# A two-layer diffusion-transformer kernel on one core: the scan's prologue moved by half a tile to a tile among the projections, its stores reordered, and a memset cut to one fifth

## The chip, the cores and the metric

The kernel runs on one core of a Trainium2 chip. The metric is the device time of one execution in microseconds; lower is better. The core has TensorE (matmuls, PE in the views), VectorE (DVE), ScalarE (ACT), GpSimd (POOL) and SyncE (SP), which here issues all the transfers. Each engine runs its own list of instructions in order, and they meet through semaphores.

## What is computed

The reference has two layers. Layer 0 mixes tokens by neighbourhood attention and a Hyena convolution, layer 1 by an RWKV-7 mixer that runs over the sequence in both directions; each layer has a SwiGLU network behind its mixer. The change lies in layer 1's mixer:

```
def rwkv_features(h, mu, w_rkv, w0, w1, w2, a0, a1, a2, g1, g2, k_k, k_a, readout):
    xx = 0.5 * (shift_prev(h) + shift_next(h)) - h
    mix = lambda i: h + xx * mu[i]
    k = mix(2) @ w_rkv[1]
    v = mix(3) @ w_rkv[2]
    ...
    kk = kk / jnp.maximum(jnp.sqrt(jnp.sum(jnp.square(kk), axis=-1, keepdims=True)), 1e-12)
    k_dir = k[None] * (1.0 + (a - 1.0) * k_a)
    if readout:
        r = mix(0) @ w_rkv[0]

def update(s, w_t, k_t, v_t, kk_t, a_t):
    sa = jnp.einsum('ebhvk,ebhk->ebhv', s, kk_t)
    return s * w_t[..., None, :] - sa[..., :, None] * (kk_t * a_t)[..., None, :] + v_t[..., :, None] * k_t[..., None, :]
```

There are 512 tokens and 256 context tokens, a width of 1024, and 16 heads of 64 in this mixer. Everything is in float32.

## The kernel before

A product with large weights is done in parts: each weight tile (128 output rows, 1024 inputs) is split by POOL into a high and a low half, and TensorE multiplies high by high, high by low and low by high. The mixer's three projections (value, key, receptance) are 24 such tiles, t = 0 to 23, eight each. A tile is eight steps k of TensorE; for receptance (t = 16 to 23) a step is three matmuls of 512 columns. For tile t: SP loads the weights (L2052) once tile t-4 is done, POOL splits them (L2184, L2186), TensorE multiplies (L1746), ACT copies the sum to one of three buffers (L1802), and SP stores it to DRAM (`keep`, L2046). In its loop SP issues the load of tile t together with `keep(t-6)`; the last six stores stand in a loop behind it.

Then the scan runs over eight pairs of heads. Its work for a pair has three parts, and round by round (`ROUNDS`) it does the back part of pair i, the front part of pair n = i+1 and the beginning of pair c = i+2. In time order for one pair:

- `kk`, `kr`: sums of the squared keys (TensorE L2450, needs the table `HONES`), their roots spread out by ACT (`kroot`, `kwide`, L2762, L2770), turned back by TensorE (L2583), and the product on DVE (`kmul`, L3029).
- `l00 l10`, `l01 l11`: two small low-rank products on TensorE (L2282), with tangents on ACT (`t00`, `t10`, ..., L2602), a gate on POOL (L2194) and prefix scans on DVE (L2803), which need the tables `RUN` and `MK`.
- exponentials and rates on ACT, products on DVE (`kin`, `ba_0`, `bt_0`, `ba_1`, `bt_1`, ..., L2808 to L2823), ending in `acc_0` on ACT (L2730).
- `A_0 A_1`: the gram matrices on TensorE (L2340), masked by DVE (L2830), sent out by SP (L2108) and brought back as 16x16 diagonal blocks (L2114), which POOL inverts by substitution (L2216, L2217). In pair 0, POOL also sets a buffer `XY` to zero (L2215) ahead of the last step. The inverses go out (L2118, L2122) and come back (L2126, L2131), and ACT and DVE expand them (L2656, L3035).
- the back part, which begins with `ta tx tb` on TensorE (L2307, L2299).

Each engine's list for the scan is a generator: a `next(scan)` in the projections' loop runs it up to its next `yield`. So the prologue (the beginning of pairs 0 and 1) is laid between projection tiles by hand. TensorE's five pieces are `kk`; `kr`; `l00 l10`; `l01 l11`; `A_0 A_1`. ACT's four are the keys' scaling and squares; `kroot kwide`; the first tangents; exponentials up to `acc_0`. SP's five are `keys_of(0) values_of(0)`; `HONES` and five small tables; `RUN` and `MK`, which wait until the stores of two buffers have landed; `queries_of(0)`; and `lora_of(1)` with the grams' way out and back. POOL's two are the gates, and an empty piece. DVE runs the scan behind its mixing, with no pieces. What is left of each list runs behind tile 23.

SP's order around the loads of the tables is this:

```
                if t >= 6:
                    keep(t - 6)
                if t in (17, 19, 21):
                    next(scan)
```

Of the kernel before, what the change touches and what calls it, by code (L numbers as in the profile page):

```python
# [84 lines left out]
def hybrid_dit_kernel(nc, a, out):  # L85
# [3 lines left out]
    with ctx:  # L89
# [1650 lines left out]
        def projections_pe(pe, scan):  # L1740

            def products(t, d, k):
                w_hi, w_lo = WH[:, t % SLOTS, k, :], WRR[:, t % SLOTS, k, :]
                for p, (wt, x) in enumerate(((w_hi, d.hi), (w_hi, d.lo), (w_lo, d.hi))):
                    for h0, h1, b in (((0, HALF, 0), (HALF, T, 1)) if d.n == T else ((0, L, 0),)):
                        last = nc.tensor.matmul(PS[:, kept_bank(t) + b, 0:h1 - h0], wt, x[:, k, h0:h1],  # L1746
                                                start=k + p == 0, stop=k == CT - 1 and p == 2)
                return last

            for k in range(CT):  # L1750
                pe.wait_ge(input_split, SPLIT_MIX + k + 1)
                for t in range(2):
                    if k == 0:
                        pe.wait_ge(lora_hid, 2)
                        pe.wait_ge(weights_split, SPLITS["value"] + t + 1)
                    last = products(t, value, k)
                    if k == CT - 1:
                        last.then_inc(slots_used, 1)
            for t, (w, d, m) in enumerate(PROJECTIONS):
                if t < 2:  # L1760
                    continue
                if t < SLOTS:
                    pe.wait_ge(lora_hid, t + 1)
                else:
                    pe.wait_ge(kept_tile, t - SLOTS + 1)
                pe.wait_ge(weights_split, SPLITS["value"] + t + 1)
                for k in range(CT):
                    if m == 0:
                        pe.wait_ge(input_split, SPLIT_MIX + d.at + k + 1)
                    last = products(t, d, k)  # L1770
                last.then_inc(slots_used, 1)
                if t in (16, 17, 18, 20):
                    next(scan)
                if t == 17:
                    next(scan)

        def projections_act(act, scan):

            def upper(d, k):
                act.wait_ge(mix_raw, d.at + k + 1)  # L1780
                if d is key and k == 0:
                    act.wait_ge(slots_used, 4 * (LORA + 1))
                if d is recept and k == 0:
                    act.wait_ge(slots_used, 4 * value.base + CT)
                nc.scalar.activation(d.hi[:, k, 0:d.n], RAW[:, (d.at + k) % 2, 0:d.n], ACT.Copy).then_inc(input_hi, 1)

            u = 4 * LORA
            for k in range(CT):
                if k == 2:
                    act.wait_ge(slots_used, u + 3)  # L1790
                    nc.scalar.activation(as_halves(TH), halves(4), ACT.Tanh).then_inc(lora_hid, 1)
                if k == 6:
                    act.wait_ge(slots_used, u + 4)
                    nc.scalar.activation(as_halves(AH), halves(6), ACT.Copy).then_inc(lora_hid, 1)
                upper(value, k)
            for t, (w, d, m) in enumerate(PROJECTIONS):
                if w < 2:
                    upper((key, recept)[w], m)
                act.wait_ge(slots_used, 4 * value.base + t + 1)
                if t >= 3:  # L1800
                    act.wait_ge(kept_out[t % 3], 16 * (t // 3))
                nc.scalar.activation(as_halves(kept_at(t), d.n), halves(kept_bank(t), d.n), ACT.Copy)\  # L1802
                  .then_inc(kept_tile, 1)
                if t in (15, 16, 17, 18):
                    next(scan)

        def mixes_sp(sp):
# [102 lines left out]
        TOKK, KINT, BVT, XY, OOS, NE = carve(ARENA[3], [2 * T, 2 * T, 2 * T, 5 * T, 5 * T, 2 * T])  # L1910
# [18 lines left out]
        XY = XY.rearrange("p (a h j t) -> p a h j t", a=5, h=2, j=6)  # L1929
# [111 lines left out]
        def projections_sp(sp, scan):  # L2041
# [14 lines left out]
                    next(scan)  # L2056
            for t in range(len(PROJECTIONS) - 6, len(PROJECTIONS)):
                keep(t)
                if t in (18, 20):
                    next(scan)  # L2060

        H2 = [slice(0, 64), slice(64, 128)]
# [115 lines left out]
        def projections_pool(pool, scan):  # L2178

            for t in range(len(PROJECTIONS)):  # L2180
# [3 lines left out]
                nc.gpsimd.tensor_copy(hi, raw).then_inc(weights_hi, 1)  # L2184
                pool.wait_ge(weights_hi, SPLITS["value"] + t + 1)
                nc.gpsimd.tensor_tensor(lo, raw, hi.bitcast(F32), ALU.subtract).then_inc(weights_split, 1)  # L2186
                if t in (20, 21):
                    next(scan)

        def scan_pool(pool):  # L2190
            sub = Chain(pool, sub_step)
# [11 lines left out]
            def substitute(n):  # L2203
                pool.wait_ge(blk_back, 32 * n + 32)
                for s in range(BK - 1):
# [6 lines left out]
                    prod = strided(PROD[:, 0:1], (256, 2), (BK, rows), (1, cols))  # L2212
                    if n == 0 and s == BK - 2:
                        pool.wait_ge(slots_used, 4 * value.base + 3 * CT)
                        sub.link(nc.gpsimd.memset(XY[:, :, :, :, :].rearrange("p a h j t -> p (a h j t)"), 0.0))  # L2215
                    sub.link(nc.gpsimd.tensor_tensor(prod, coef, done, ALU.mult))  # L2216
                    ins = nc.gpsimd.tensor_tensor(rest, rest, prod, ALU.subtract)  # L2217
                    if s < BK - 2:
# [1056 lines left out]
```

## Time and profile before

| | us |
|---|---|
| three timed runs | 2462.48, 2462.98, 2466.24 (median 2462.98) |
| the profiled execution | 2464.82 |
| its span, from the first to the last instruction | 2463.0 |
| TensorE busy | 2216.2 (90% of the span) |
| VectorE, ScalarE, GpSimd busy | 942.2, 688.3, 852.2 |

The profile is one execution. Its page gives the busy time of each engine and groups of instructions by line; the trace behind it answers questions on a stretch: what ran when on one engine (the timeline), what ended the idle time in front of an instruction (in brackets), and busy time and granted TensorE clock by stretch. All times are microseconds from the start of the span.

### The profile page before, as it was taken

The numbers are of one execution on the slowest core, as the hardware profiler recorded it, in microseconds if no ns is written. First come the engines' busy times: TensorE is split into PE (matmuls) and PEld (weight loads), VectorE is DVE, ScalarE is ACT, GpSimd is POOL, SyncE is SP. The second block draws the span as 40 slices with busy tenths as digits, with TensorE's granted clock in tenths as the row PEclk, the third lists the DMA queues.
The fourth block names the chain that finished last, engine by engine and source line by source line (L and its number), as shares of the span: only waits on it lengthen the run. The fifth ranks groups of instructions, "written<-read, shape, count | busy, mean of one in ns | idle before, by whom it ended". The sixth has DMA issues, their size and how long they took to land. (4 is left out here: it accounts for less than half of the span.)

```text
span 2463.0 us, 50823 instructions
## 1 busy us (share of the span) xinstructions
PE 2216.2 (90%) x22528; PEld 1842.0 (75%) x22528; DVE 942.2 (38%) x1500; ACT 688.3 (28%) x1059; POOL 852.2 (35%) x692
## 2 busy tenths in 40 slices
PE   5899989989699999999958998888888887999997
PEld 3788765555399999999926996777776665888785
DVE  3102265990320000022289214777777524000123
ACT  4110166421320000022232123555555223101112
POOL 2132300000233443434306445333333243666662
PEclk8999999999799999999979999999999988999998
DMA  6555530001012112111112444323233131222221
GB/s 247 214 192 215 194 135 18 1 8 69 26 52 68 60 60 68 60 60 60 45 37 77 118 131 116 65 56 59 56 63 62 23 117 55 94 94 94 85 99 64
DMA packets 175508, 210.32 MB, mean 85 GB/s; under 512 B 124791, under 2 KB 133751, under 8 KB 168152
## 3 DMA queue, kind: packets, MB, share of 16 engines
q1 hardware_dynamic: 175320, 207.49, 27.3%
q8 instruction: 157, 2.57, 0.4%
q14 instruction: 31, 0.25, 0.0%
HBM read 184.65 MB, written 22.81 MB: 84 GB/s over the span
## 5 line engine op out<-in xcount | busy, mean ns | idle before, releaser
L254 POOL CAST TMP_r<-WR 128x1024 fp32r<-128x1024 f32 x120 | 127.2, 1060 | 718.4 <-DMA WR<-in_ffn_w_dram 437.1
L273 PE MATMUL PS<-H_r,TMP_r 128*128 128x384 f32 (+1 forms) x1088 | 330.2, 359 | 11.6 <-DVE Y_r L490 11.6
L273 PE MATMUL PS<-Y_r,TMP_r 128*128 128x384 f32 (+1 forms) x1088 | 329.9, 358 | 3.7 <-DVE H_r L490 3.7
L256 POOL TENSOR_TENSOR WR_r<-WR,TMP_r 128x1024 fp32r<-128x1024 f32 x120 | 289.2, 2410 | 9.6
L413 DVE TENSOR_TENSOR P<-TMP,PS 128x768 f32 (+1 forms) x44 | 36.1, 821 | 562.5 <-PE PS L273 562.5
L273 PEld LDWEIGHTS PS<-H_r,TMP_r 128*128 128x128 f32 x1088 | 202.5, 190 | 28.3 <-DVE Y_r L490 12.6
L273 PEld LDWEIGHTS PS<-Y_r,TMP_r 128*128 128x128 f32 x1088 | 201.3, 189 | 19.3 <-DVE H_r L490 4.0
L273 PE MATMUL PS<-H_r,WR_r 128*128 128x384 f32 x736 | 191.6, 342 | 0.0
L396 ACT ACTIVATE TMP<-PS 128x768 f32<-128x768 f32 (+1 forms) x44 | 31.0, 705 | 526.1 <-PE PS L273 526.1
L590 PE MATMUL PS<-H_r,TMP_r 128*128 128x384 f32 x704 | 151.9, 338 | 3.2 <-DVE H_r L628 2.2
L273 PE MATMUL PS<-Y_r,WR_r 128*128 128x512 f32 x352 | 139.2, 396 | 0.0
L273 PEld LDWEIGHTS PS<-H_r,WR_r 128*128 128x128 f32 x736 | 133.4, 189 | 0.0
L590 PEld LDWEIGHTS PS<-H_r,TMP_r 128*128 128x128 f32 x704 | 125.5, 189 | 3.8 <-DVE P L413 2.5
L1746 PE MATMUL PS<-P_r,TMP_r 128*128 128x384 f32 (+1 forms) x448 | 114.2, 347 | 6.7 <-POOL WR_r L2186 4.3
L2216 POOL TENSOR_TENSOR scan_small<-scan_small 96x30 f32<-96x30 f32 (+7 forms) x120 | 49.7, 414 | 191.3 <-DMA scan_small<-gram_dram 182.6
L590 PE MATMUL PS<-Y_r,TMP_r 128*128 128x512 f32 x352 | 109.7, 393 | 2.2 <-DVE Y_r L628 2.2
L266 POOL TENSOR_TENSOR WR_r<-WR,TMP_r 128x1024 fp32r<-128x1024 f32 x44 | 107.2, 2437 | 3.5
L1629 PE MATMUL PS<-H_r,TMP_r 128*128 128x384 f32 x352 | 93.4, 347 | 8.6 <-POOL WR_r L256 8.6
L264 POOL CAST TMP_r<-WR 128x1024 fp32r<-128x1024 f32 x44 | 47.3, 1074 | 154.7 <-DMA WR<-in_down_dram 154.7
L2184 POOL CAST TMP_r<-WR 128x1024 fp32r<-128x1024 f32 x24 | 42.1, 1756 | 151.3 <-DMA WR<-in_rw_w_rkv_dram 151.3
L628 DVE TENSOR_TENSOR H_r<-P,H_r 128x768 fp32r<-128x768 f32 x44 | 44.2, 1043 | 125.7 <-ACT H_r L621 125.7
L1746 PE MATMUL PS<-P_r,WR_r 128*128 128x384 f32 (+1 forms) x320 | 91.3, 350 | 0.0
(327 smaller groups left out, 4468.0 us busy)
## 6 DMA issues: line engine op xcount, KB each, us to landing
WR<-in_ffn_w_dram SPq DMA_DIRECT2D x88, 512.0 KB, 3.4
TMP<-in_mod_w_dram SPq DMA_DIRECT2D x40, 1024.0 KB, 4.8
WR<-in_down_dram SPq DMA_DIRECT2D x44, 512.0 KB, 3.4
WR<-in_mix_w_in_dram SPq DMA_DIRECT2D x24, 512.0 KB, 6.9
WR<-in_rw_w_rkv_dram SPq DMA_DIRECT2D x24, 512.0 KB, 4.2
P<-in_mod_w_dram SPq DMA_DIRECT2D x4, 2048.0 KB, 22.0
vkr_dram<-extra SPq DMA_DIRECT2D x16, 384.0 KB, 4.8
scan_front<-vkr_dram SPq DMA_DIRECT2D x16, 384.0 KB, 3.6
```

Source lines behind the costliest of these rows:

```text
L254: nc.gpsimd.tensor_copy(hi, raw).then_inc(weights_hi, 1)
L256: nc.gpsimd.tensor_tensor(lo, raw, hi.bitcast(F32), ALU.subtract).then_inc(weights_split, 1)
L264: nc.gpsimd.tensor_copy(hi, raw).then_inc(weights_hi, 1)
L266: nc.gpsimd.tensor_tensor(lo, raw, hi.bitcast(F32), ALU.subtract).then_inc(weights_split, 1)
L273: last = nc.tensor.matmul(PS[:, bank + b, 0:h1 - h0], w, x[:, h0:h1], start=k + p == 0, stop=k == CT - 1 and p == 2)
L413: nc.vector.tensor_tensor(as_halves(dst, d.n), as_halves(GATE[:, u, 0:d.n], d.n), halves(4 * u + 2, d.n), ALU.mult).then_inc(d.unit_free, 1)
L590: last = nc.tensor.matmul(PS[:, bank, 0:h1 - h0], w[:, at:at + 128], x[:, q % 4, h0:h1], start=k + p == 0, stop=k == FT - 1 and p == 2)
L628: nc.vector.tensor_tensor(d.lo[:, q % 4, :], P[:, q % FT, 0:d.n], d.hi[:, q % 4, :].bitcast(F32), ALU.subtract).then_inc(hid_split, 1)
L1629: last = nc.tensor.matmul(PS[:, 2 * u + b, 0:HALF], w, x[:, HALF * b:HALF * b + HALF], start=k + p == 0, stop=k == CT - 1 and p == 2)
L1746: last = nc.tensor.matmul(PS[:, kept_bank(t) + b, 0:h1 - h0], wt, x[:, k, h0:h1], start=k + p == 0, stop=k == CT - 1 and p == 2)
L2184: nc.gpsimd.tensor_copy(hi, raw).then_inc(weights_hi, 1)
L2216: sub.link(nc.gpsimd.tensor_tensor(prod, coef, done, ALU.mult))
```

## The change

It moves where the pieces of the prologue are run, and cuts one memset.

- TensorE: `kk` moves from behind tile 16 to behind step k = 3 of tile 16; `kr` and `l00 l10` from behind tile 17 to behind tile 16; `l01 l11` from behind tile 18 to behind step k = 3 of tile 17; `A_0 A_1` from behind tile 20 to behind tile 19.
- ACT: its four pieces move from behind the evictions of tiles 15, 16, 17, 18 to behind those of 15, 15, 16, 17.
- SP: `queries_of(0)` stays behind `keep(18)`, and the piece with the grams, which stood behind `keep(20)`, follows it at once, ahead of `keep(19)` to `keep(23)`. The pieces at t = 17, 19, 21 stay.
- POOL: the gates move from behind the split of tile 20 to behind that of tile 19. The memset of `XY` covers one of its five parts, `XY[:, 4]`.

```diff
--- before.py
+++ after.py
@@ -1768,10 +1768,12 @@
                     if m == 0:
                         pe.wait_ge(input_split, SPLIT_MIX + d.at + k + 1)
                     last = products(t, d, k)
+                    if t in (16, 17) and k == 3:
+                        next(scan)
                 last.then_inc(slots_used, 1)
-                if t in (16, 17, 18, 20):
+                if t in (16, 19):
                     next(scan)
-                if t == 17:
+                if t == 16:
                     next(scan)
 
         def projections_act(act, scan):
@@ -1801,7 +1803,9 @@
                     act.wait_ge(kept_out[t % 3], 16 * (t // 3))
                 nc.scalar.activation(as_halves(kept_at(t), d.n), halves(kept_bank(t), d.n), ACT.Copy)\
                   .then_inc(kept_tile, 1)
-                if t in (15, 16, 17, 18):
+                if t in (15, 16, 17):
+                    next(scan)
+                if t == 15:
                     next(scan)
 
         def mixes_sp(sp):
@@ -2056,7 +2060,8 @@
                     next(scan)
             for t in range(len(PROJECTIONS) - 6, len(PROJECTIONS)):
                 keep(t)
-                if t in (18, 20):
+                if t == 18:
+                    next(scan)
                     next(scan)
 
         H2 = [slice(0, 64), slice(64, 128)]
@@ -2184,7 +2189,7 @@
                 nc.gpsimd.tensor_copy(hi, raw).then_inc(weights_hi, 1)
                 pool.wait_ge(weights_hi, SPLITS["value"] + t + 1)
                 nc.gpsimd.tensor_tensor(lo, raw, hi.bitcast(F32), ALU.subtract).then_inc(weights_split, 1)
-                if t in (20, 21):
+                if t in (19, 20):
                     next(scan)
 
         def scan_pool(pool):
@@ -2212,7 +2217,7 @@
                     prod = strided(PROD[:, 0:1], (256, 2), (BK, rows), (1, cols))
                     if n == 0 and s == BK - 2:
                         pool.wait_ge(slots_used, 4 * value.base + 3 * CT)
-                        sub.link(nc.gpsimd.memset(XY[:, :, :, :, :].rearrange("p a h j t -> p (a h j t)"), 0.0))
+                        sub.link(nc.gpsimd.memset(XY[:, 4].rearrange("p h j t -> p (h j t)"), 0.0))
                     sub.link(nc.gpsimd.tensor_tensor(prod, coef, done, ALU.mult))
                     ins = nc.gpsimd.tensor_tensor(rest, rest, prod, ALU.subtract)
                     if s < BK - 2:
```

## Rows read from the trace of the kernel before

**Rows 1.** The page, its first part: busy time of each engine.

```profile
PE 2216.2 (90%) x22528; PEld 1842.0 (75%) x22528; DVE 942.2 (38%) x1500; ACT 688.3 (28%) x1059; POOL 852.2 (35%) x692
```

**Rows 2.** Busy time by stretch: length, PE, PEld, DVE, ACT, POOL, clock, DMA share, GB/s.

```profile
1315.00:1514.50 199.50, 191.50 (x1099) 178.80 (x1098) 78.01 (x80) 48.18 (x68) 91.34 (x59) 0.98 0.39 112
1514.50:1540.10 25.60, 14.73 (x313) 12.15 (x312) 9.22 (x15) 12.40 (x19) 18.63 (x28) 0.89 0.36 74
```

**Rows 3.** Timeline of TensorE: start, length, line, operation, count, idle before.

```profile
1461.79 0.39 PE L1746 MATMUL PS<-P_r,TMP_r 128*128 128x512 f32 x1
...
1467.62 1.47 PE L2450 MATMUL PS<-scan_front 128*128 128x2 f32 x12 [0.19 <-DMA scan_front<-in_headones_dram]
...
1474.52 0.82 PE L2583 MATMUL PS<-ident,scan_front 128*128 128x128 f32 x6
1476.43 1.56 PE L2282 MATMUL PS<-TMP,scan_small 64*128 64x384 f32 x8 [1.09 <-issue]
...
1496.17 1.85 PE L2340 MATMUL PS<-scan_tokens,scan_front 64*64 64x64 f32 x96
...
1514.49 0.93 PE L2329 MATMUL PS<-scan_front,scan_tokens 64*64 64x64 f32 x48
...
1531.93 1.56 PE L2282 MATMUL PS<-TMP,scan_small 64*128 64x384 f32 x8 [1.38 <-DVE scan_front L2857]
1540.13 1.56 PE L2307 MATMUL PS<-scan_back,scan_tokens 64*64 64x64 f32 x48 [6.64 <-ACT scan_back L2656]
```

**Rows 4.** Timeline of VectorE.

```profile
1483.38 4.00 DVE L2803 TENSOR_TENSOR_SCAN scan_front<-extra,scan_front 128x768 f32<-128x768 f32 x2 [7.05 <-DMA extra<-in_grammask_dram]
...
1495.36 1.68 DVE L2815 SCALAR_TENSOR_TENSOR scan_front<-scan_front 128x768 f32<-128x768 f32 x1
...
1547.45 1.79 DVE L2797 TENSOR_TENSOR scan_small<-scan_back,PS 128x768 f32<-128x768 f32 x2
```

**Rows 5.** Timeline of ScalarE.

```profile
1470.13 0.84 ACT L2770 ACTIVATE scan_front<-scan_small 128x768 f32<-128x768 f32 x1 [0.58 <-DVE scan_small L3017]
...
1537.95 2.13 ACT L2656 ACTIVATE scan_back<-scan_back,scan_small 128x384 f32<-128x384 f32 x4 [9.01 <-DMA scan_back<-inv_dram]
...
1541.50 0.90 ACT L2602 ACTIVATE scan_front<-PS,PC 128x768 f32<-128x768 f32 x1
```

**Rows 6.** Timeline of GpSimd.

```profile
1512.17 0.23 POOL L2216 TENSOR_TENSOR scan_small<-scan_small 96x30 f32<-96x30 f32 x1 [12.22 <-DMA scan_small<-gram_dram]
...
1526.40 3.31 POOL L2215 MEMSET scan_back<- 128x3840 f32 x1
```

**Rows 7.** Timeline of SyncE: its DMA issues.

```profile
1462.83 0.43 SPq L2092 DMA_DIRECT2D scan_front<-in_headones_dram  x1
...
1474.71 0.33 SPq L2052 DMA_DIRECT2D WR<-in_rw_w_rkv_dram  x1
1475.08 0.43 SPq L2046 DMA_DIRECT2D vkr_dram<-extra  x1
1479.81 0.33 SPq L2100 DMA_DIRECT2D extra<-in_run_dram  x1
...
1503.21 3.35 SPq L2108 DMA_DIRECT2D gram_dram<-scan_tokens  x4
```

**Rows 8.** DMA issues, 1455 to 1545 us: count, KB, median us to landing.

```profile
extra<-in_grammask_dram SPq DMA_DIRECT2D x1, 128.0 KB, 3.1
...
scan_front<-in_headones_dram SPq DMA_DIRECT2D x1, 64.0 KB, 4.7
```

**Rows 9.** Lines L2803 and L2808: duration ns min/median/max, first and last start.

```profile
L2803 DVE TENSOR_TENSOR_SCAN scan_front<-extra,scan_front x16: 1726/1758/2354, 1483.4 to 1887.7; 128x768 f32<-128x768 f32 x16
...
L2808 DVE TENSOR_TENSOR scan_tokens<-scan_front x16: 936/940/3146, 1488.3 to 1894.1; 128x756 f32<-128x756 f32 x16
```

**Rows 10.** Busy time by stretch, around the start of round 0; columns as in rows 2.

```profile
1538.00:1539.00 1.00, 0.00 (x0) 0.00 (x0) 0.00 (x0) 1.00 (x3) 0.00 (x0) 0.56 0.75 67
...
1544.00:1545.00 1.00, 1.00 (x48) 1.00 (x47) 1.00 (x1) 0.72 (x1) 1.00 (x1) 0.53 0.72 261
```

## The prediction, made before the change was run

> **What bounds the kernel now.** The page says that TensorE is busy for 90% of the span [rows 1], but that is an average. I read it by stage next [rows 2]: the projections (to 1514.5 us) keep TensorE busy 191.5 of 199.5 us, the passage into the scan (1514.5 to 1540.1) only 14.7 of 25.6. All that the change touches lies in these two. Eight scan rounds follow, each hanging on the one before, so I take a shift of round 0 as a shift of the end. The question is: when can round 0 (`ta`, L2307) start?
>
> TensorE runs in order, and two chains end there. The **inversion chain**: SP sends the masked grams at 1503.21 [rows 7], POOL substitutes from 1512.17 [rows 6], the result goes out again, ACT expands it from 1537.95 [rows 5], and `ta` starts at 1540.13. The **front chain**: after the last projection tile TensorE does all of head pair 0's turns and grams and pair 1's `kk`, `kr` and `l00 l10`; it starts at 1514.49, and its last link starts at 1531.93 and takes 1.5 us [rows 3]. So before, 6.64 us of idle lie behind the front chain [rows 3], and the inversion chain decides. The change shortens the inversion chain; that can win 6.6 us at most, if the front chain doesn't move. My claim is that the front chain moves, and by more.
>
> **Part 1, `kk` in the middle of tile 16.** It needs `HONES`. SP issues that load at 1462.83, in the step behind the end of tile 15 [rows 7], and it takes 4.7 us to land [rows 8]: 1467.5. Before, `kk` stood behind tile 16 and waited 0.19 us for it [rows 3]. A tile of 24 matmuls takes 5.4 us (from 1461.79 on, with its last matmul's pipeline 5.6). Now TensorE reaches `kk` after 12 of them, at 1464.6, and stands still until 1467.6 with tile 16's second half and all later tiles queued behind. Idle grows by 2.9 us. `kk` holds TensorE for 1.3, the second half takes 3.0: tile 16 ends at 1471.9, where it ended at 1467.4.
>
> **Part 2, `kr` and `l00 l10` behind tile 16, `l01 l11` in tile 17.** ACT's `kwide`, which `kr` needs, is through at 1471.0 [rows 5], and is no earlier now, since `kk` isn't. `kr` (0.8 us), the wait for DVE's product (1.1, as before) and `l00 l10` (1.5) [rows 3] now lie ahead of tile 17, which starts at 1475.2. Its halves (2.8 and 3.0) with `l01 l11` (1.5) between them end at 1482.5. Before, it had none of this ahead of it and ended at 1474.7. So **tile 17 ends 7.8 us later**: 2.9 of stall, and 3.4 and 1.5 of small work moved ahead of it. Moved work by itself costs TensorE nothing.
>
> **Part 3, the load that hangs on tile 17.** SP's step t=21 is not changed: it waits for the end of tile 17, issues a weight load and `keep(15)`, and the scan's next step waits for that store to land before it loads `RUN` and `MK` over its buffer. Before: 1474.71, 1475.08, then 1479.81 [rows 7] and 3.1 us from `MK`'s issue to its landing [rows 8]. DVE's two prefix scans need both and had waited 7.05 us for them [rows 4]. Now the same steps run 7.8 us later: `RUN` goes out at 1487.6, and the scans start at **1491.2 instead of 1483.4**. The gates on POOL come earlier (behind tile 19's split, not 20's), but DVE wasn't waiting for them.
>
> **Part 4, the grams behind tile 19.** `A_0` and `A_1` need `bt_0` and `bt_1` of DVE. `bt_1` ended 13.7 us after the scans' start, at 1497.04 [rows 4]. Now that is 1491.2 + 13.7 = 1504.9. The unknown is how far POOL's weight splits stretch DVE. Before, the two scans took 4.00 where the median is 1.76 each, and `bt_1` 1.68 where products of its size take 0.94 [rows 4, 9]: 1.2 us on this path. One product was stretched from 0.94 to 3.15, 2.2 us. Two splits still fall here (tiles 22 and 23, on the second scan and on `ba_0`). I take the old sum; without any stretch it is 1503.7, with one in full 1505.9, with two 1508.1. TensorE has ended tile 19 at 1493.3 and idles until `bt_0` at about 1503. `A_1`, half of the grams' 1.85 us, takes 0.9, and tile 20 starts at 1506.0 with the handover. Before, the grams ran from 1496.17 to 1498.0 [rows 3] and three tiles came behind them; now four do. The end of tile 23 moves by 8.0 + 5.4 = **13.4 us**.
>
> **The clock.** Behind the 6.64 us of idle before `ta` the granted clock falls to half, the lower of the two levels (1.2 GHz): the slice from 1538 has 0.56, that from 1544 still 0.53 [rows 10], so the lower level lasts some 4.4 us into the work. The new idle of 9 us is longer. Half of those 4.4 us is lost where the work is dense; `A_0` and the wait for `bt_1` hide part. I take 1.2 us, with 0 and 2.2 as bounds. Sum for tile 23: **14.6 us**. The Trainium skill (TensorE: Matmul & The Clock Gate, Part 1) says that an idle array falls to half its clock and sustained work frees it again; the trace agrees (0.53 and 0.56). It speaks against any edit that opens a gap in dense work; a clock that stayed up would leave the sum at 2467.8.
>
> **Part 5, what follows tile 23.** The rest of the front chain keeps its length: its links wait for tile 23, for the last store, and for `keys_of(1)`, whose load SP issues behind that store. So `l00 l10` of pair 1 starts at 1531.9 + 14.6 = 1546.5, ACT's first tangent at 1548.0 instead of 1541.50 [rows 5], and `ta` at 1548.0 instead of 1540.13. The old idle is used up. From there it is DVE's first sweep (1547.45 before, right behind a scan [rows 4]) that counts: tangent 0.9, eviction of `ta` 0.8, tangent 0.9, gate 0.85, scan 1.8 put it at 1553.4. **Round 0's dense part comes 6.0 us later.** `ta`, `tx` and `tb` ran at the low clock before and now run mostly warm; that is why it is 6.0 and not 7.9.
>
> **Part 6, the inversion chain, now covered.** ACT runs its fourth step ahead of evicting tile 18. It waits there for the scans, and the evictions of tiles 18 and 19 are queued behind it until `acc_0` (about 1506.5); their banks are needed only by tiles 22 and 23, later. `keep(18)` waits for them too. SP issues it, `queries_of(0)` and two small loads (2.0 us) and sends the grams at about 1509, not 1503.2. `keep(19)` to `keep(23)` queue behind the grams' return, and have time, since their tiles end later. Substitution starts 9.0 us behind the sending [rows 6, 7], at 1518. The memset shrinks to a fifth: 3.31 us for 3840 columns [rows 6] becomes 0.7, which saves 2.6. The expansion could begin at 1541.3, but ACT's `kwide` for pair 1, ahead of it, ends at 1543.4. `ta` at 1548.0 waits for neither. So the memset edit is worth nothing here; with the front chain on time it would be worth its 2.6 us.
>
> **Rival A, the move works (2456.4).** If neither load is late, the prologue runs a tile earlier: the inversion chain gains 5.4 and 2.6, the front chain doesn't move, and `ta` gains the 6.6 us of idle. For it: TensorE's work is the same in sum. Against it: `HONES` and `RUN` stay issued behind the ends of tiles 15 and 17, and DVE's wait of 7.05 us for the latter is in the trace. It decides if the scans start before 1483. Chance 0.12.
>
> **Rival B, the delay is half hidden (2466.6).** No stretch (-1.2) and no cold clock (-1.2): tile 23 moves 12.2 and round 0 3.6. Further slack in round 0 would take it towards 2463. For it: one stretched product, of 3.15 us, lay where DVE waited for ACT anyway. Against it: both splits are still to be done. Chance 0.33.
>
> **Rival C, more contention (2472.4).** `RUN` and `MK` now go out half a microsecond ahead of tile 22's weight load and a store: up to 1.6 us more, if they land like the 4.7 us of rows 8. With one stretch in full (+1.0) and the full cold price (+1.0) that is 3.4 to 3.6 us over the main case; with two stretches 2474.6. Chance 0.12.
>
> By the Trainium skill (GPSIMD Engine Reference, the table at its head) GpSimd shares its memory interface with DVE where a DVE instruction has two inputs in SBUF, as the scans and products here have. The stretched product agrees.
>
> **How the numbers follow.** The profiled span is 2463.0 us (that execution took 2464.8; the median of three is 2462.98, so I add to the median as it is): 2463.0 + 6.0 = **2469.0 us**, +0.24%. This case by itself spans 2467 to 2472 and has chance 0.43. The range that should hold 8 in 10 takes in rival B with its slack and all of C but its end: 2459 to 2474. About 0.2% (4.9 us) is what a measurement of this kernel can tell from no change. The main case and C lie above it, B inside, A below: slower 0.55, same 0.33, faster 0.12.
>
> **What the profile after would show.** Right: a wait of 3 us ahead of L2450 within tile 16; `RUN` issued near 1487.6 and L2803 starting near 1491; TensorE idle some 9 us ahead of L2340; the last L1746 near 1528; hardly any idle ahead of `ta`; a memset of 0.7 us. Wrong: L2803 before 1484, L2340 right behind tile 19, or several microseconds of idle left ahead of `ta`, which would mean that the inversion chain still decides.

## The result, and the profile after

| | before | after |
|---|---|---|
| median | 2462.48 us | 2474.28 us |
| lowest and highest (7 runs each) | 2454.77, 2466.24 | 2467.21, 2478.70 |
| the profiled execution, its span | 2464.82, 2463.0 | 2470.45, 2468.7 |

The ratio is 1.0046 [1.0030, 1.0061]: the change makes the kernel **11.3 us slower**, between 7.4 and 15.0. The forecast was +6.0. The direction and the way were right; the size was about half of the measured one, and the median of after lies at the upper end of the range (2474), 0.3 us above it. It is also outside the 2467 to 2472 that the main case spans by itself: as a number it is nearest to rival C (2472.4, at its end 2474.6).

The profiled execution of after, 2470.45, is close to the 2469.0 forecast, but that is no confirmation. The work upstream of the change varies between executions. Tile 16 starts at 1461.79 before [rows 3], and after it starts at 1456.14, 5.65 us sooner, with nothing changed ahead of it. All distances below are therefore taken **from the start of tile 16 of the same execution**.

TensorE in the profile of after, the same places as in rows 3 (start, length, line, operation, shape, count, idle before and its releaser; these lines of the kernel are numbered 5 higher):

```profile
1456.14 0.39 PE L1746 MATMUL PS<-P_r,TMP_r 128*128 128x512 f32 x1
...
1462.22 1.47 PE L2455 MATMUL PS<-scan_front 128*128 128x2 f32 x12 [3.16 <-DMA scan_front<-in_headones_dram]
...
1465.11 0.63 PE L1746 MATMUL PS<-Y_r,TMP_r 128*128 128x512 f32 x1
1465.54 0.63 PE L1746 MATMUL PS<-P_r,WR_r 128*128 128x512 f32 x1
...
1467.98 0.81 PE L2588 MATMUL PS<-ident,scan_front 128*128 128x128 f32 x6
...
1500.48 1.56 PE L2345 MATMUL PS<-scan_tokens,scan_front 64*64 64x64 f32 x48 [10.77 <-DVE scan_front L2820]
1502.34 1.56 PE L2345 MATMUL PS<-scan_tokens,scan_front 64*64 64x64 f32 x48 [0.30 <-DVE scan_front L2820]
1503.83 0.79 PE L1746 MATMUL PS<-P_r,TMP_r 128*128 128x512 f32 x1
...
1525.98 0.39 PE L1746 MATMUL PS<-P_r,WR_r 128*128 128x512 f32 x1
...
1535.37 2.54 PE L2455 MATMUL PS<-scan_front 128*128 128x2 f32 x12 [2.41 <-ACT scan_front L2763]
...
1540.50 2.48 PE L2372 MATMUL PS<-scan_tokens,scan_front 64*64 64x64 f32 x96
...
1545.52 2.67 PE L2287 MATMUL PS<-TMP,scan_small 64*128 64x384 f32 x8 [1.38 <-DVE scan_front L2862]
1548.12 1.41 PE L2312 MATMUL PS<-scan_back,scan_tokens 64*64 64x64 f32 x48
```

Three of the forecast signs stand in it. `kk` waits 3.16 us in the middle of tile 16, where it had waited 0.19 [rows 3]. The grams wait 10.77 us behind tile 19, where there was no wait. Behind the front chain `ta` starts at 1548.12 with no idle at all, where there had been 6.64 us [rows 3]. And VectorE shows where the grams' wait is from:

```profile
1487.43 3.41 DVE L2808 TENSOR_TENSOR_SCAN scan_front<-extra,scan_front 128x768 f32<-128x768 f32 x2 [17.64 <-DMA extra<-in_grammask_dram]
1491.74 3.95 DVE L2813 TENSOR_TENSOR scan_tokens<-scan_front 128x756 f32<-128x756 f32 x2 [0.91 <-ACT scan_front L2611]
1495.62 1.78 DVE L2817 SCALAR_TENSOR_TENSOR scan_front<-scan_front 128x768 f32<-128x768 f32 x1
1497.44 2.98 DVE L2820 SCALAR_TENSOR_TENSOR scan_front<-scan_front 128x768 f32<-128x768 f32 x1
1500.35 0.94 DVE L2817 SCALAR_TENSOR_TENSOR scan_front<-scan_front 128x768 f32<-128x768 f32 x1
1501.33 0.96 DVE L2820 SCALAR_TENSOR_TENSOR scan_front<-scan_front 128x768 f32<-128x768 f32 x1
...
1554.20 1.79 DVE L2802 TENSOR_TENSOR scan_small<-scan_back,PS 128x768 f32<-128x768 f32 x2
```

The scans wait 17.64 us for their tables (7.05 in rows 4). SyncE's issues name the step that sends the tables late: the weight load and the store behind the end of tile 17, and the wait for that store.

```profile
1457.18 0.43 SPq L2097 DMA_DIRECT2D scan_front<-in_headones_dram  x1
...
1478.86 0.33 SPq L2056 DMA_DIRECT2D WR<-in_rw_w_rkv_dram  x1
1479.23 0.43 SPq L2050 DMA_DIRECT2D vkr_dram<-extra  x1
1484.01 0.33 SPq L2105 DMA_DIRECT2D extra<-in_run_dram  x1
```

What stood at 12.9, 13.3 and 18.0 us behind the start of tile 16 [rows 7] now stands at 22.7, 23.1 and 27.9.

The windows of after (length, PE, PEld, DVE, ACT, POOL, clock, DMA share, GB/s) hold something that the forecast had missed:

```profile
1464.00:1466.00 2.00, 2.00 (x7) 1.51 (x6) 0.57 (x2) 0.84 (x1) 0.33 (x1) 0.50 0.00 0
```

Most of the second half of tile 16 runs at a granted clock of 0.50, the lower of the two levels, with matmuls 0.43 us apart instead of 0.23. The 3.16 us ahead of `kk` are paid as a wait, and then more is lost to the low clock, in the densest part of the kernel.

### The profile page after: what moved, and what is told of

It is laid out like the page before. It is cut to its first block and busy times, and to the rows that moved or that the text cites. A ratio compares the mean times of both kernels' runs of the same rounds, so it can differ in the third digit from the quotient of the medians.

```text
span 2468.7 us, 50823 instructions
## 1 busy us (share of the span) xinstructions
PE 2213.2 (90%) x22528; PEld 1843.5 (75%) x22528; DVE 943.7 (38%) x1500; ACT 688.6 (28%) x1059; POOL 848.1 (34%) x692
## 5 line engine op out<-in xcount | busy, mean ns | idle before, releaser
L273 PE MATMUL PS<-H_r,TMP_r 128*128 128x384 f32 (+1 forms) x1088 | 331.1, 360 | 11.1 <-DVE Y_r L490 11.1
L396 ACT ACTIVATE TMP<-PS 128x768 f32<-128x768 f32 (+1 forms) x44 | 31.1, 706 | 524.8 <-PE PS L273 524.8
## 6 DMA issues: line engine op xcount, KB each, us to landing
P<-in_mod_w_dram SPq DMA_DIRECT2D x4, 2048.0 KB, 21.6
```

What stands on the lines that cost most here:

```text
L273: last = nc.tensor.matmul(PS[:, bank + b, 0:h1 - h0], w, x[:, h0:h1], start=k + p == 0, stop=k == CT - 1 and p == 2)
```

## Where the 12.4 us of the profile come from

All in microseconds behind the start of tile 16:

| | before | after | moved | forecast |
|---|---|---|---|---|
| scans start | 21.6 | 31.3 | +9.7 | +7.8 |
| grams done, next tile starts (21 before, 20 after) | 36.2 | 47.7 | +11.5 | +8.0 |
| last matmul of tile 23 starts | 52.4 | 69.8 | +17.5 | +14.6 |
| `l00 l10` of pair 1 start | 70.1 | 89.4 | +19.2 | +14.6 |
| `ta` starts | 78.3 | 92.0 | +13.6 | +7.9 |
| first sweep on DVE | 85.7 | 98.1 | +12.4 | +6.0 |

The first sweep is DVE's first product of round 0 (L2797 before, L2802 after). From there on the two kernels take the same within some 1 us (915.6 us to the end of the span before, 914.5 after), so the row of the sweep is the row to read.

## The experiments

Three theories stood at the start. **Late loads**: `HONES` and `RUN` stay where they were, and the moved pieces wait for them. **Inversion chain**: it still sets the start of `ta`, as it did before. **Moved work**: the small pieces cost something by being cut into the tiles. A fourth, **low clock**, that part of the time is lost to matmuls at the lower level, came with the profile of after. Each kernel was timed beside the kernel before on the same chip, 5 rounds; "sweep" is how far the first sweep has moved against the profile of before, and "ratio" is the timed one. A sweep comes from one execution. The change measured a second time, **e13_change_again**, shows how much that is worth:

> The changed kernel once more, for a second profile and a second ratio, taken with the same runs of the kernel before as the three others. The part of the front chain behind tile 23, up to l00 l10 of pair 1, took 19.5 us in its first profile, 17.8 before the change and 16.0 to 18.8 in other versions, with the granted clock at half in more or fewer of its pieces. If that is a matter of where the clock happens to fall, it will differ again here, by up to 2 us, with the same program; the stall ahead of kk (3.0), the scans' start (31) and the gap ahead of the grams (10.8) will be the same. The ratio to before again 1.003 to 1.006.

Measured: 1.0045 [1.0028, 1.0062], 11.1 us, with the sweep at +10.3, where the first profile had +12.4. The ratios agree to 0.2 us, the two profiles differ by 2. TensorE again, in this second profile:

```profile
1463.39 1.47 PE L2455 MATMUL PS<-scan_front 128*128 128x2 f32 x12 [2.86 <-DMA scan_front<-in_headones_dram]
...
1501.46 1.56 PE L2345 MATMUL PS<-scan_tokens,scan_front 64*64 64x64 f32 x48 [10.58 <-DVE scan_front L2820]
...
1536.23 1.86 PE L2455 MATMUL PS<-scan_front 128*128 128x2 f32 x12 [1.98 <-ACT scan_front L2763]
...
1545.97 1.56 PE L2287 MATMUL PS<-TMP,scan_small 64*128 64x384 f32 x8 [1.38 <-DVE scan_front L2862]
```

The waits are the same within 0.3 us. What differs is the tail: `kk` of pair 1 takes 1.86 instead of 2.54 and `l00 l10` 1.56 instead of 2.67. So single profiles are good to some 2 us here, and smaller differences between them are not read.

The table of all kernels; positions are us behind the start of tile 16.

| kernel | scans start | last matmul of tile 23 | `ta` | sweep moved | ratio |
|---|---|---|---|---|---|
| before | 21.6 | 52.4 | 78.3 | | |
| the change | 31.3 | 69.8 | 92.0 | +12.4 | 1.0046 [1.0030, 1.0061] |
| e13_change_again | 30.9 | 69.7 | 89.9 | +10.3 | 1.0045 [1.0028, 1.0062] |
| e1_hones_early | 26.5 | 65.9 | 84.9 | +5.3 | 1.0030 [1.0016, 1.0044] |
| e2_run_early | 21.3 | 59.7 | 80.0 | +0.4 | 0.9995 [0.9984, 1.0007] |
| e3_both_early | 16.6 | 56.2 | 77.2 | -2.4 | 0.9990 [0.9978, 1.0002] |
| e4_grams_after_20 | 31.2 | 64.4 | 85.8 | +7.4 | 1.0026 [1.0013, 1.0039] |
| e5_full_memset | 31.1 | 69.9 | 90.1 | +10.6 | 1.0039 [1.0022, 1.0055] |
| e6_memset_alone | 21.8 | 52.5 | 77.0 | -1.3 | 0.9995 [0.9982, 1.0008] |
| e7_stores_alone | 21.6 | 52.7 | 77.0 | -1.4 | 0.9991 [0.9977, 1.0004] |
| e12_stores_and_memset | 21.6 | 52.3 | 73.9 | -4.4 | 0.9988 [0.9975, 1.0001] |
| e9_loads_early_grams_20 | 16.9 | 51.9 | 72.4 | -5.9 | 0.9967 [0.9954, 0.9980] |
| e10_before_all_but_pe | 17.7 | 51.8 | 72.3 | -7.2 | 0.9963 [0.9948, 0.9979] |
| e11_gaps_filled | 31.7 | 71.2 | 88.7 | +9.1 | 1.0035 [1.0022, 1.0049] |

### The load of HONES one step sooner

e1_hones_early is the change with one number altered; the step with `HONES` now stands behind the end of tile 14, not 15:

```diff
-                if t in (17, 19, 21):
+                if t in (17, 18, 21):
                     next(scan)
```

> The changed kernel, with SP's step that loads HONES moved from t = 19 to t = 18, so that the table is there when TensorE reaches kk in the middle of tile 16. RUN and MK stay behind tile 17. Front-chain theory (the end of the front chain on TensorE sets round 0, and the stall inside tile 16 and the low clock behind it are 4.8 of its delay): no stall ahead of kk, tile 16's second half at full clock, the scans start 26.5 us behind the start of tile 16 (31.3 in the changed kernel, 21.6 before), and the whole runs 4.8 us faster than the change, which leaves it about 6.5 us slower than before. Inversion-chain theory (the late sending of the grams sets round 0): the grams go out 4.8 us earlier too, so the same total, but TensorE is idle for several us ahead of ta. Rival that TensorE loses by interrupting a tile's accumulation: kk still costs more than its 1.3 us, and less than 2 us come back.

Measured: sweep +5.3, ratio 1.0030, 7.4 us. By the ratios 3.9 us came back (the two intervals overlap), by the profiles 5 (from the second profile of the change) to 7. `kk` does not wait (TensorE of e1):

```profile
1463.88 1.50 PE L2455 MATMUL PS<-scan_front 128*128 128x2 f32 x12
1468.09 0.82 PE L2588 MATMUL PS<-ident,scan_front 128*128 128x128 f32 x6
```

Its first row and its second are 4.21 us apart; in the change the same two are 5.76 apart (1462.22 and 1467.98). The difference, **1.6 us, is the price of the low clock** in tile 16's second half, since this kernel's clock is 1.00 there (window, columns as above). It repeats: the distance is 5.75 or 5.76 us in all five profiles in which `kk` waits some 3 us in the middle of tile 16 (the change twice, e2, e4, e5), and 4.20 or 4.21 in the three in which it doesn't wait there (e1, e3, e9).

```profile
1463.00:1465.00 2.00, 2.00 (x15) 1.65 (x14) 0.00 (x0) 1.98 (x2) 0.00 (x0) 1.00 0.76 266
```

The wait and the low clock together are 4.7 us, and the scans come 4.8 sooner than in the change. The wait ahead of the grams is as long as it was (10.76): early or late, tile 19 and the scans move together, since the load of `RUN` hangs on tile 17. Cutting tile 16 in two costs next to nothing by itself: of the 4.21 us `kk` takes 1.4, and the second half of the tile 2.8, like the first.

### The loads of RUN and MK one step sooner

```diff
-                if t >= 6:
+                if t >= 6 and t != 21:
                     keep(t - 6)
-                if t in (17, 19, 21):
+                if t == 20:
+                    keep(15)
+                if t in (17, 19, 20):
                     next(scan)
```

> The changed kernel, with the store of tile 15 issued at t = 20 behind that of tile 14, and RUN and MK loaded in that step instead of t = 21. HONES stays late. Front-chain theory: the stall in tile 16 stays (3 us, and 1.8 of low clock), but the scans start about 20.6 us behind the start of tile 16 instead of 31.3, the gap of 10.8 us ahead of the grams shrinks to under 1, tile 23 ends about 12 us earlier than in the change, and round 0 starts 15 us earlier: about 2 us faster than before. Inversion-chain theory: the grams go out earlier by as much, and the same comes out. Rival that the load of RUN was no cause: nothing comes back.

Measured: sweep +0.4, ratio 0.9995, 1.2 us faster than before, with an interval that takes in 1. Against the change some 12 us came back by either measure (+11.3 to -1.2; +12.4 to +0.4). This is the largest single part of the loss, and what was put right is SyncE's step, which the change does not touch. TensorE of e2:

```profile
1464.36 1.47 PE L2457 MATMUL PS<-scan_front 128*128 128x2 f32 x12 [2.86 <-DMA scan_front<-in_headones_dram]
...
1491.77 0.93 PE L2347 MATMUL PS<-scan_tokens,scan_front 64*64 64x64 f32 x48
1495.71 0.93 PE L2347 MATMUL PS<-scan_tokens,scan_front 64*64 64x64 f32 x48 [3.02 <-DVE scan_front L2822]
```

`A_0` no longer waits. `A_1` still waits 3.02 for `bt_1`, and yet it runs at the full clock (0.93 us).

### Both loads sooner

e3_both_early is e2 with `(17, 18, 20)`.

> The changed kernel with both loads early (HONES at t = 18, the store of tile 15 and RUN and MK at t = 20). Front-chain theory: no stall in tile 16, scans some 16 us behind the start of tile 16, no gap ahead of the grams, tile 23 ends where it ended before, and round 0 starts right behind the front chain, with the old idle of 6.6 us ahead of ta used up: 6 to 8 us faster than before (2455). It can't be more than about 8.5. If the inversion chain is what sets round 0, idle is left ahead of ta and the gain is smaller.

Measured: sweep -2.4 and 0.9990 [0.9978, 1.0002], 2.5 us with an interval that takes in 1, less than was expected. The waits for both loads are gone (`kk` has none), and the scans start 5.0 us sooner than before. What is late next is `A_1`. TensorE and VectorE of e3:

```profile
1485.46 0.93 PE L2347 MATMUL PS<-scan_tokens,scan_front 64*64 64x64 f32 x48
1489.25 1.56 PE L2347 MATMUL PS<-scan_tokens,scan_front 64*64 64x64 f32 x48 [2.86 <-DVE scan_front L2822]
```

```profile
1481.12 2.36 DVE L2819 SCALAR_TENSOR_TENSOR scan_front<-scan_front 128x768 f32<-128x768 f32 x1 [0.73 <-ACT scan_front L2626]
1483.51 0.96 DVE L2822 SCALAR_TENSOR_TENSOR scan_front<-scan_front 128x768 f32<-128x768 f32 x1
1484.39 1.79 DVE L2819 SCALAR_TENSOR_TENSOR scan_front<-scan_front 128x768 f32<-128x768 f32 x1
1486.21 2.98 DVE L2822 SCALAR_TENSOR_TENSOR scan_front<-scan_front 128x768 f32<-128x768 f32 x1
```

The four products before `A_1` take 8.1 us; 0.95 is what each takes undisturbed (`ba_1` and `bt_1` of after). GpSimd splits weights beside three of them. `A_1` then runs at the low clock (1.56 instead of 0.93), and the beginning of tile 20 too: 2.86 + 0.6 + 0.5 makes 4.0, and tile 23 is 3.9 us later than in before. In e2 the same piece waited 3.02 us and kept the full clock, so a wait of this length does not always cost a low clock; what decides it was not found. The loads early are not sufficient: with `A_0 A_1` behind tile 19 the product chain on DVE ends some 3 us too late. This kernel is also the test of rival A, the change with neither load late: it gives 2.5 us and not the rival's 6.6.

### The grams behind tile 20, as they were

e4_grams_after_20 is the change with the loads late and this edit; e9 has the early loads as well.

```diff
-                if t in (16, 19):
+                if t in (16, 20):
                     next(scan)
```

> The changed kernel, with TensorE's grams behind tile 20, where they were before, and all else as in the change. Tells the two chains apart: the grams can't run earlier than DVE's products allow, so SP sends them at the same time, but one more tile fills the gap in front of them. Front-chain theory: the gap shrinks from 10.8 to about 5 us, tile 23 and round 0 come 5.5 to 6 us earlier, so that it is 5 to 6 us slower than before. Inversion-chain theory: the sending of the grams and with it round 0 stay where they are, and it stays 11 us slower than before.

Measured: the wait ahead of `A_0` falls from 10.77 to 5.39, a tile's length; sweep +7.4; ratio 1.0026, 6.4 us. By the ratios 4.9 us came back, by the profiles 2.9 to 5.0. The gap is shorter by one tile, and by no more. The run also tells the two chains apart. SyncE sends the grams 50.1 us behind the start of tile 16, where the change has 50.5, and still `ta` comes 6.2 us sooner (4.1 against the second profile of the change): in the change the front chain sets its start and not the inversion chain.

> The kernel with both loads early, and TensorE's grams behind tile 20 as before the change. With the grams behind tile 19, A_1 had waited 2.9 us for bt_1 and ran at the low clock, and tile 23 ended 3.9 us later than before the change. Front-chain theory: the wait is gone, tile 23 ends where it did before the change (52.7 us behind the start of tile 16), nothing is idle ahead of ta, and DVE's first sweep comes 77 to 79 us behind the first receptance matmul, where it was 85.4 before and 83.1 with the grams behind tile 19: 6 to 8 us faster than before. If the inversion chain decides by now, idle is left ahead of ta and it is 2 to 4 us faster only.

Measured: 0.9967 [0.9954, 0.9980], **8.1 us faster than before**; sweep -5.9. No piece that TensorE runs among the projections waits for a load, and the grams do not wait for DVE:

```profile
1495.95 1.63 PE L2347 MATMUL PS<-scan_tokens,scan_front 64*64 64x64 f32 x96
```

### The kernel before, with everything but the moves on TensorE, ScalarE and GpSimd

e10 is the kernel before with e3's edit of SyncE's loop, SyncE's last two pieces together, and the small memset:

```diff
                 keep(t)
-                if t in (18, 20):
+                if t == 18:
+                    next(scan)
                     next(scan)
...
-                        sub.link(nc.gpsimd.memset(XY[:, :, :, :, :].rearrange("p a h j t -> p (a h j t)"), 0.0))
+                        sub.link(nc.gpsimd.memset(XY[:, 4].rearrange("p h j t -> p (h j t)"), 0.0))
```

> The kernel before with the change's two parts on the inversion chain (the grams sent ahead of the last stores, the small memset) and both loads early, but with no piece of the prologue moved on TensorE, ACT and POOL. If the half-tile steps themselves are worth something, this is slower than the version with them and both loads early (grams behind tile 20). Front-chain theory: it is as fast, 5 to 8 us faster than before, since the scans start some 19 us behind tile 16's start (21.6 before), the grams go out some 5 us earlier and the memset gives 2.6, up to the front chain's end. Rival: the scans wait for POOL's gates, which come late, and it stays within 3 us of before.

Measured: 0.9963 [0.9948, 0.9979], **9.1 us faster than before**, with a sweep of -7.2; the lowest ratio here. It and e9 differ by the moves of `kk`, `kr`, `l00 l10`, `l01 l11` alone (and their gates and exponentials), and their intervals overlap almost wholly: these moves have no gain of their own that was measured. TensorE and VectorE of e10:

```profile
1494.98 1.63 PE L2343 MATMUL PS<-scan_tokens,scan_front 64*64 64x64 f32 x96
...
1530.46 2.93 PE L2285 MATMUL PS<-TMP,scan_small 64*128 64x384 f32 x8 [1.38 <-DVE scan_front L2860]
1533.32 1.17 PE L2310 MATMUL PS<-scan_back,scan_tokens 64*64 64x64 f32 x48
```

```profile
1478.68 4.81 DVE L2806 TENSOR_TENSOR_SCAN scan_front<-extra,scan_front 128x768 f32<-128x768 f32 x2 [3.57 <-POOL scan_front L2197]
```

The scans now wait 3.57 us for GpSimd's gate and no longer for a load. That is not seen on TensorE: the grams run in one block with no wait. `ta` follows the front chain directly, so the inversion chain is no longer the bound; the front chain is, with `l00 l10` at the low clock (2.93 us where 1.56 is the full-clock time).

### The memset and the stores

e5_full_memset is the change with the whole of `XY` set to zero again.

> The changed kernel with the whole memset of before (3.3 us and not 0.7). Front-chain theory: the inversion chain has some 2 to 6 us to spare in the changed kernel, so it makes no difference to the change (within 1 us; 11 us slower than before). Inversion-chain theory: 2.6 us slower than the change.

Measured: 1.0039 [1.0022, 1.0055], sweep +10.6: no difference from the change can be told, as the forecast's Part 6 has it. With the front chain late the memset's length is covered.

On the kernel before the inversion chain is the bound, so there both edits should count. e6 has the memset's edit alone, e7 the order of SyncE's pieces alone, e12 both.

> The kernel before with the small memset alone. Before the change the inversion chain decides, with 6.6 us of idle on TensorE ahead of ta. Two-chain theory: the memset takes 0.7 us instead of 3.3, the idle ahead of ta shrinks by 2.6 and it is 2.6 us faster than before. Rival (the transfers of the inverses decide, or POOL's last steps aren't on the path): no difference.

> The kernel before with the grams sent ahead of the last stores alone. Before, SP came to the grams at 41.2 us behind the first receptance matmul, after two stores and two small loads that waited for ACT's late evictions, while the first masked gram was ready at about 39. Two-chain theory: the grams go out about 2 us earlier, substitution starts 2 us earlier, and it is 2 us faster than before. Rival: the stores now behind the grams delay the load of the next keys, and nothing is gained.

> The kernel before with the change's two parts on the inversion chain together: the grams ahead of the last stores and the small memset, and no piece moved on TensorE, ACT and POOL. Two-chain theory: the gains add, 2 + 2.6 = 4.6 us faster than before, with some 2 us of idle left ahead of ta. It tells how much of the 8 to 9 us of the version that also has its loads early is due to these two parts: about half.

Measured: the sweep moves by -1.3, -1.4 and -4.4 us, the ratios say -1.2, -2.2 and -3.0, each with an interval that takes in 1. So neither edit has a gain clear of the noise, alone or with the other. The forecast's "worth its 2.6 us" for the memset is neither shown nor ruled out: e6's profile gives 1.3, e12 against e7 gives 3.0, and the timed interval of e6 runs from 4.4 us faster to 2.0 slower. In e6's execution part of the gain was lost on the way. SyncE in before and in e6, the way out and back of the inverses:

```profile
1531.56 0.81 SPq L2118 DMA_DIRECT2D inv_dram<-scan_small  x2
...
1533.73 2.08 SPq L2126 DMA_DIRECT2D scan_back<-inv_dram  x2
```

```profile
1529.69 0.82 SPq L2118 DMA_DIRECT2D inv_dram<-scan_small  x2
...
1533.03 1.97 SPq L2126 DMA_DIRECT2D scan_back<-inv_dram  x2
```

Behind tile 16's start the first of these rows is at 69.8 and 67.3, so 2.4 us did arrive there; the last is at 71.9 and 70.7, and 1.3 is left. The return goes out 3.3 us behind the store instead of 2.2. Why the store's way took longer in this execution is not settled. With both edits the idle ahead of `ta` is down to 0.81 us, waiting for ScalarE, and the front chain is next.

### The gaps filled with work that keeps TensorE busy

e11_gaps_filled is the change with transposes of the identity put where TensorE would idle: 20 ahead of `kk`, 70 ahead of `A_0`. Their results are overwritten by what follows.

```diff
+                    if c == 0:
+                        for _ in range(20):
+                            nc.tensor.transpose(PS[:, b, 0:128], ident[:, :], ident[:, :])
...
+                    if n == 0:
+                        b = front("A_0", n)
+                        for _ in range(70):
+                            nc.tensor.transpose(PS[:, b, 0:128], ident[:, :], ident[:, :])
```

> The changed kernel with TensorE's two new gaps filled by transposes of the identity whose results are overwritten: 20 ahead of kk in tile 16 and 70 ahead of A_0, in the bank that comes next. No wait is shortened, so it tells the low clock's price from that of the waits. Theory: the granted clock stays at the full level, tile 16's second half takes 2.7 us and not 4.4 (1.8 back), A_1 and tile 20's first matmuls another 1.3; together 3 us faster than the change, 8 us slower than before. If the clock's fall has another cause than TensorE's idleness, nothing comes back.

Measured: 1.0035 [1.0022, 1.0049], 8.6 us, sweep +9.1. TensorE and the windows of e11 in tile 16:

```profile
1464.54 2.40 PE L2569 MATMUL PS<-ident 128*128 128x128 f32 x20
1467.66 1.50 PE L2455 MATMUL PS<-scan_front 128*128 128x2 f32 x12 [0.72 <-DMA scan_front<-in_headones_dram]
...
1473.45 0.82 PE L2595 MATMUL PS<-ident,scan_front 128*128 128x128 f32 x6
...
1500.14 9.71 PE L2502 MATMUL PS<-ident 128*128 128x128 f32 x70 [4.96 <-ACT scan_front L2614]
1509.78 1.63 PE L2345 MATMUL PS<-scan_tokens,scan_front 64*64 64x64 f32 x96
```

```profile
1465.00:1467.00 2.00, 1.94 (x18) 1.70 (x16) 0.00 (x0) 0.78 (x1) 0.61 (x1) 1.00 0.98 340
...
1470.00:1472.00 2.00, 2.00 (x6) 1.53 (x6) 0.15 (x1) 0.84 (x1) 0.00 (x0) 0.50 0.00 0
```

In tile 16 the theory fell in the form it was put. Only 0.72 us of idle is left, TensorE is busy in the records, and still the clock drops to 0.50 and the second half takes as long (`kk` to `kr`: 5.79 us, against 5.76 in the change and 4.21 in e1). Narrow matmuls back to back did not hold the clock there. So e1 shows that the low clock goes away with the wait for the load, and that TensorE's idleness in it is the cause is not shown. Ahead of the grams they did bring it back: the second filler waited 4.96 us for ScalarE to read its bank out, ran 70 transposes in 9.71, and the grams (1.63 for all 96, where the change needs 1.56 for 48) and tile 20 ran at the full clock. But it overran: `bt_0` had ended at 1506.5 and `A_0` starts at 1509.78. So tile 23 comes 1.4 us later than in the change. In this profile the sweep is sooner all the same, since the front chain takes 16.0 us (last matmul of tile 23 to `l00 l10`), the shortest of all kernels: 17.8 before, 19.5 and 18.7 in the two profiles of the change. By the ratios its 8.6 us and the change's 11.3 and 11.1 have overlapping intervals, so that the fillers gain anything is not shown.

## Why the prediction was right, and why its size was not

**Right.** The reading that two chains end at `ta`, and that the front chain moves by more than the 6.64 us of idle [rows 3] ahead of it; e4 shows that it sets `ta` in the change. (That the idle is all that can be won fits e9 and e10 by their profiles, 5.9 and 7.2, and by their timed intervals, which begin at 4.9 and 5.2 us.) The wait of 2.9 us for `HONES` (3.16 and 2.86 measured). `RUN` hanging on tile 17, shown by e2, which gives 12 us back with SyncE's step alone. The grams' idle ("some 9 us", measured 10.77). Part 6: the memset worth nothing in this kernel (e5), `ta` with no idle ahead. (SyncE sent the grams 50.5 us behind the start of tile 16 where Part 6 has 47.2, which stayed covered.) Rival A, that neither load is late, is out, and its 6.6 us would not have come either: e3, with both loads on time, gains 2.5 us by its ratio, since `A_1` then waits for DVE. Only with the grams back behind tile 20 as well do 8.1 us come (e9).

**Too small.** The forecast for the sweep was +6.0, the profile has +12.4. Term by term:

- **Part 1 left the clock out: +1.6.** It counted what an idle of 9 us does to the clock and took the 2.9 us ahead of `kk` as a plain wait. e1 puts the price at 1.6 us. The stall itself is 0.2 longer than forecast, and tile 17 is longer by 0.2 for its extra handover. Together: scans +9.7 instead of +7.8.
- **Part 4, the products: +1.2.** From the start of the scans to the end of `bt_1` it took 14.9 us, not 13.7. The forecast's sum with one product stretched in full (+1.0) comes within 0.2 us of that, but it was put in rival C, and belonged in the main case. In the trace the stretch is spread: 3.95 us for the two products of L2813, 1.78 for `ba_0`, 2.98 for `bt_0`, while the scans (3.41) and `bt_1` (0.96) took less than before.
- **The clock behind the gap: as forecast.** `A_1` takes 0.6 more and tile 20 0.5 more at the low level, 1.1 us against 1.2. Here tile 23 stands at +17.5 instead of +14.6.
- **Part 5 said that the front chain keeps its length: +1.8.** From tile 23's last matmul to `l00 l10` it was 17.8 before and is 19.5 here, 18.7 in the second profile. Its links are the same. `kk` takes 1.0 longer (2.54 in one profile, 1.86 in the other, 1.50 at the full clock) and the grams behind it 0.4; another 0.4 is wait ahead of `kk`, since the load of `keys_of(1)` went out 4.45 us behind the start of tile 23's last matmul instead of 4.05. (The rows of before stand behind this list.)
- **`l00 l10` at the low clock: +1.1**, 2.67 instead of 1.56; in the second profile it ran at the full clock. That, and 0.6 us less regained between `ta` and the sweep than forecast, makes 2.9 + 1.8 + 1.1 + 0.6 = 6.4, the whole miss. In the second profile of the change the same sum is 2.7 + 0.9 + 0 + 0.7 = 4.3: the part up to tile 23 repeats, and the part behind it was 3.5 us in one execution and 1.6 in the other.

```profile
1523.15 1.55 PE L2450 MATMUL PS<-scan_front 128*128 128x2 f32 x12 [2.00 <-ACT scan_front L2758]
...
1527.29 1.90 PE L2367 MATMUL PS<-scan_tokens,scan_front 64*64 64x64 f32 x96
```

Before the change the low clock in the front chain cost nothing, because 6.64 us of idle lay behind it. The forecast knew that this cover was gone, and charged it for the delay of tile 23, but not for the chain's own low clock. By the ratio, which is the better measure, +11.3 against +6.0 leaves 5.3 us, with an interval from 1.4 to 9.0: it would be the 2.9 to the end of tile 23, and 2.4 of the 3.5 behind it. That the tail differs by 2 us between two profiles of the same kernel fits, and what decides which of its pieces the low clock hits was not found.

Rival B took both unknowns, the stretch and the cold clock, at their good end. The stretch came out at one product in full, the clock behind the gap as forecast, and the low clock in two places that were not listed came on top. Rival C has nearly the measured number (2472.4), but not for its reasons: of its three terms only the stretch came true. `RUN` and `MK` landed no later than before (the scans start 3.4 us behind the issue of `RUN`, 3.6 before), and the clock behind the gap cost 1.1 us and not the full price. The two places that nobody listed made up for both, which is luck.

The Trainium skill (TensorE: Matmul & The Clock Gate, Part 1) says that activity is what releases the clock. For wide matmuls the traces agree: the second half of tile 16 is at the full level again before it ends (the granted clock is 0.50 from 1464 to 1466, 0.67 on average from 1466 to 1468, and 1.00 behind that). In e11 narrow matmuls kept TensorE busy ahead of `kk`, and the clock fell all the same.

## What to carry to other kernels

When a step is moved earlier, look up every load that it waits for and ask which event that load's issue hangs on: here the loads of two tables and one store, issued a step sooner in SyncE's loop, gave back 12 us. Then look up what it waits for next: with the loads on time the grams waited for DVE's products. Charge a wait that opens in dense work once for its length, and leave room in the range for the matmuls behind it at half clock (here 1.6 us behind the wait of `kk`, 1.1 behind that of `A_1` in e3, nothing behind that of `A_1` in e2). And when an edit uses up the idle time behind a chain, recount the chain itself, since what was covered in it now shows.

## What the runs showed of the hardware that was not expected

- Behind a stall of 3.16 us and twelve 2-column products the granted clock fell to 0.50, which cost another 1.6 us. In before and in e1 the same products without the stall left it at 1.00. Behind stalls of 2.86 us (e3) and 3.02 us (e2) ahead of `A_1` it was 0.50 once and 1.00 once.
- Twenty 128-column transposes in the gap ahead of `kk`, with 0.72 us of idle left, did not keep the clock up; seventy of them in a longer gap brought it back to 1.00.
- The load of `HONES`, 64 KB, took 4.9 us to land in the change, where it went out 0.9 us behind the issue of a weight load of 512 KB, with a store of 384 KB between them. In e1 it went out 2.1 us behind the same pair and took 3.1 us.
- Beside GpSimd's weight splits (2.93 and 3.15 us for a subtraction of 128x1024) a product on DVE takes 2.98 instead of 0.96, two of them 3.95 instead of 1.9. By the Trainium skill (GPSIMD Engine Reference, Specifications) GpSimd's memory interfaces are shared with VectorE, with contention where a VectorE instruction has two inputs in SBUF; these have two, and the trace agrees.
